# A layer with routed experts on one core: the first pair's first half ahead of its last rows, and the final sums tile by tile

## What is computed

```
h = x + concat(a, c) @ w_out                 # 1024 x 1024
xn = rms_norm(h, g_norm_ffn)
lg = xn @ w_router_group;  g = argmax(lg)    # 4 groups
le = xn @ w_router_expert                    # 8 experts in the group; the best two are taken
w_sel = softmax(top_v) * p_g
y = h + sum over the two experts of w_sel * (silu(xn @ w_gate[e]) * (xn @ w_up[e])) @ w_down[e]
```

## Time and profile before

| | us |
|---|---|
| median of 3 runs | 611.67 |
| lowest and highest | 610.62, 613.29 |
| the profiled execution's own time | 607.84 |
| its span, first to last instruction | 606.1 |
| TensorE busy in the span | 553.9 |
| VectorE, ScalarE, GpSimd busy | 278.1, 166.8, 119.2 |
| mean granted clock of TensorE | 0.965 |
| bytes moved by DMA | 163.48 MB |

### The profile page before, as it was taken

The page is one execution under the profiler, slowest core; times in us unless marked ns, Lnnn a source line. Parts: engine busy times, 40 slices in busy tenths (PEclk is TensorE's granted clock), DMA queues, the critical chain, the costliest instruction groups (busy, mean ns, idle before and its releaser), DMA issues.

```text
span 606.1 us, 8209 instructions
## 1 busy us (share of the span) xinstructions
PE 553.9 (91%) x2944; PEld 332.5 (55%) x2944; DVE 278.1 (46%) x681; ACT 166.8 (28%) x365; POOL 119.2 (20%) x124
## 2 busy tenths in 40 slices
PE   6999999998999999899999999999996869687992
PEld 4798899887675888744555853333332313232320
DVE  5887667968314787524358731111210111111256
ACT  7445344423312567610412210100100100000031
POOL 0488788310001000000000021111110111100013
PEclk9999999999999999899999999999997979898897
DMA  7990342599377900069600879999999999999874
GB/s 274 281 304 5 118 156 66 183 273 316 143 209 251 420 31 2 2 203 407 264 35 36 355 250 388 409 419 419 422 421 421 421 419 421 420 422 419 333 297 156
DMA packets 47159, 163.48 MB, mean 270 GB/s; under 512 B 8650, under 2 KB 22026, under 8 KB 35832
## 3 DMA queue, kind: packets, MB, share of 16 engines
q1 hardware_dynamic: 40448, 145.46, 63.2%
q0 software_dynamic: 6528, 17.01, 7.8%
q10 hardware_dynamic: 144, 0.52, 0.2%
HBM read 151.06 MB, written 19.76 MB: 282 GB/s over the span
## 4 chain that ended last, share of the span: by engine, by line
PE 47%; SPq 17%; DMA 11%; DVE 6%; POOL 3%; issue 3%; ACT 2%; POOLq 0%; DVEq 0%; ACTq 0%
SPq L512 11%; PE bank L1022 9%; PE bank L1085 9%; SPq L525 6%; DMA ring<-in_w_up_dram 5%; PE bank L1112 4%; PE bank L875 4%; DMA x<-q_rows 3%; PE bank L786 3%; PE bank L860 2%; DVE x L1445 2%; PE bank L808 2%; POOL ring L2139 2%; DMA hn_rows<-work 2%; PE bank L809 2%
## 5 line engine op out<-in xcount | busy, mean ns | idle before, releaser
L1085 PE MATMUL bank<-ring,work 128*64 128x512 f32 x512 | 122.8, 636 | 19.8 <-DMA ring<-in_w_up_dram 19.5
L1085 PEld LDWEIGHTS bank<-ring,work 128*64 128x64 f32 x512 | 39.6, 146 | 100.9 <-issue 87.1
L1445 DVE TENSOR_TENSOR work<-work,bank 128x256 f32<-128x256 f32 x16 | 6.7, 422 | 134.0 <-ACT work L1383 134.0
L1112 PE MATMUL bank<-ring,work 128*64 128x512 f32 x256 | 60.1, 612 | 7.6 <-ACT work L1387 7.6
L729 PE MATMUL bank<-split 128*128 128x384 f32 x192 | 66.1, 344 | 0.1
L730 PE MATMUL bank<-split 128*128 128x384 f32 x192 | 64.3, 335 | 0.0
L1022 PE MATMUL bank<-ring 128*128 128x512 f32 x96 | 42.6, 595 | 0.0
L1383 ACT ACTIVATE work<-bank 128x256 f32<-128x256 f32 x16 | 6.2, 385 | 128.2 <-PE bank L1085 128.2
L2139 POOL TENSOR_TENSOR ring<-ring 128x192 f32<-128x192 f32 (+1 forms) x40 | 38.8, 988 | 8.0 <-DVEq L1540 6.9
L1445 DVE TENSOR_TENSOR split<-ring,split 128x768 fp32r<-128x768 f32 (+1 forms) x35 | 37.3, 1099 | 6.4 <-PE bank L716 6.1
L1112 PEld LDWEIGHTS bank<-ring,work 128*64 128x64 f32 x256 | 17.3, 140 | 40.1 <-issue 28.7
(11 more groups left out here) (266 smaller groups left out, 832.9 us busy)
## 6 DMA issues: line engine op xcount, KB each, us to landing
ring<-in_w_down_dram SPq DMA_DIRECT2D x32, 1024.0 KB, 24.5
ring<-in_w_gate_dram SPq DMA_DIRECT2D x28, 1024.0 KB, 23.1
ring<-in_w_up_dram SPq DMA_DIRECT2D x28, 1024.0 KB, 25.2
ring<-in_w_in_dram SPq DMA_DIRECT2D x7, 1536.0 KB, 11.4
results<-work POOLq DMA_DIRECT2D x1, 4160.0 KB, 26.1
x<-in_x_prompt_dram SPq DMA_DIRECT2D x8, 512.0 KB, 13.1
ring<-in_w_out_dram SPq DMA_DIRECT2D x1, 4096.0 KB, 17.9
ring<-in_w_gate_dram SPq DMA_DIRECT2D x8, 512.0 KB, 13.2
```

Source lines behind the costliest of these rows:

```text
L1085: last = pe.matmul(bank[2][64 * h:64 * h + 64, :], xgT[:, k, 64 * h:64 * h + 64], gate_up[s][h][:, :, k, :], start=(k == 0), stop=(k == KD ...
L1112: last = pe.matmul(bank[4 + j][64 * h:64 * h + 64, :], hT[:, c, 64 * h:64 * h + 64], down[s][h][:, c, j * 512:(j + 1) * 512], start=(c == ...
L1445: return dve.tensor_tensor(out, a, b, op)
```

## The change

Six things, which belong together in two places.

1. `wout` is two tensors of 512 columns, loaded by two DMAs. The even groups g use only the first, so SP issues the first gate and up loads of pair 2 at `op_done` 18 and no longer at 19.
2. `hn[4]` lies at float 4096, not 3072. `tokens(0)` no longer waits for its store; the wait goes to those who first write `yo[0]`, which lies there (`result` on VectorE and ScalarE's copy, for pair 0).
3. The chunks 0 to 3 of all tiles go ahead. Then VectorE evacuates bank 0 and TensorE runs the first four chunks of pair 0; the chunks 4 to 7 and `tabulate` follow within `pair(0)`, ahead of its second half. `pick(2)` stands ahead of `choose(3)`.
4. x of tiles 1 and 2 is multiplied by the identity into PSUM (`own_row`): two products after pair 13, with four small ones (`keep_warm`) behind them, one ahead of pair 15's `pair_down`, one in the final sums. The holder's product is added in PSUM, and `add_sum` goes.
5. The final sums go tile by tile in the order 0, NT, 1, 2, 3, both halves of a tile together. ScalarE and GpSimd scale and add tiles 1 and 2 by halves.
6. The last tile's store is issued by ScalarE.

```diff
-        wout = cut(ring, 2 * SLOT, KD, D)
+        wout = [cut(ring, 2 * SLOT + j * 4096, KD, 512) for j in range(2)]
-        hn = [cut(work, at, D) for at in (0, D, 0, D, 3 * D)]
+        hn = [cut(work, at, D) for at in (0, D, 0, D, 4 * D)]
+        FINAL = [0, NT, 1, 2, 3]
+        SUM_BANKS = {0: (2, 3), NT: (4, 5), 1: (6, 7), 2: (0, 1), 3: (2, 3)}
...
+            sp.wait_ge(S["op_done"], 4 * NT + 2)
+            gates((4, 5), 2, (0,))
             sp.wait_ge(S["op_done"], 4 * NT + 3)
-            gates((4, 5), 2, (0,))
             downs((4, 5), 2)
...
                 for k in range(KD):
+                    if first and k == KD // 2:
+                        for m in range(1, T5):
+                            pick_rows(m, high_half)
+                        for b in range(len(GROUPS)):
+                            tabulate(b)
...
+            def own_row(t, half):
+                pe.matmul(sum_bank(t, half)[:, :], ident[:, :], x[:, t, half * 512:(half + 1) * 512], start=True, stop=False)
             for i in range(13, 16):
...
+                else:
+                    own_row(SUMMED[1], 0)
                 pair_down(i, s, i // 3 + 1, False, i == PAIRS - 1)
+                if i == 13:
+                    own_row(SUMMED[0], 0)
+                    own_row(SUMMED[0], 1)
+                    keep_warm(4, bank[3])
...
-            for half in range(2):
-                pe.wait_ge(S["dn_evac_v" if half else "dn_evac_a"], PAIRS)
-                for m, t in enumerate(LAST):
...
+            for m, t in enumerate(FINAL):
+                if t == SUMMED[1]:
+                    own_row(t, 1)
+                for half in range(2):
+                    if m == 0:
+                        pe.wait_ge(S["dn_evac_v" if half else "dn_evac_a"], PAIRS)
+                    if t == FINAL[-1]:
+                        pe.wait_ge(*((S["h_done"], T5 + 1) if half else (S["add_read"], 1)))
+                    pe.matmul(sum_bank(t, half)[0:TILES[t], :], holder[:, t, 0:TILES[t]], yo[0][:, half * 512:(half + 1) * 512],
+                              start=(t not in SUMMED), stop=True).then_inc(S["added"], 1)
...
-                if isinstance(i, int) and i == 0:
-                    dve.wait_ge(rows_moved[ORDER[NT]], 16)
...
             read_ranks(2)
+            pick(2)
             r_copy(4)
             choose(3)
-            pick(2)
             read_ranks(3)
             pick(3)
             place(2)
+            tokens(0, gains[:, 22:30], (0,))
             place(3)
...
-            tokens(0, gains[:, 22:30])
+            tokens(0, gains[:, 22:30], (1,))
...
+                if t in SUMMED:
+                    dve.wait_ge(S["back_summed"], 2 * SUMMED.index(t) + half + 1)
+                    rows = back[t][:, 0, cols]
+                else:
+                    rows = x[0:n, t, cols]
+                tt(x[0:n, t, cols], rows, sum_bank(t, half)[0:n, :], ALU.add).then_inc(S["h_done" if half else "add_read"], 1)
...
+            act.wait_ge(S["h_done"], 2 * T5)
+            act.dma_start(y_rows[FINAL[-1]], x[:, FINAL[-1], :]).then_inc(S["y_out"], 16)
```

More of the change, by code:

```diff
@@ L387, in placed, with sum_bank @@
             return first[m] + n
-        def add_bank(k):
-            return bank[(0, 1, 6, 7, 2, 3, 4, 5, 0, 1)[k]]
+        def sum_bank(t, half):
+            return bank[SUM_BANKS[t][half]]
         T5 = NT + 1
@@ L498, in _ @@
             sp.wait_ge(S["blk_done"], 6)
-            sp.dma_start(wout, w_out_v).then_inc(S["wout_in"], 16)
+            for j in range(2):
+                sp.dma_start(wout[j], w_out_v[:, :, j * 512:(j + 1) * 512]).then_inc(S["wout_in"], 16)
             sp.wait_ge(S["v_used"], 2)
@@ L909, in _ @@
                 last.then_inc(S["a_turned"], 1)
[L910 removed]
+            pe.wait_ge(S["wout_in"], 32)
             pe.wait_ge(S["a_evac"], 2 * NT + 1)
@@ L1003, in _ @@
                     q = k // 2
-                    last = pe.matmul(bank[6 + j][32 * q:32 * q + 32, :], mixsT[:, k, :], wout[:, k, j * 512:(j + 1) * 512],
+                    last = pe.matmul(bank[6 + j][32 * q:32 * q + 32, :], mixsT[:, k, :], wout[j][:, k, :],
                                      start=(k % 2 == 0), stop=(k % 2 == 1))
@@ L1021, in out_group @@
                         src = attnT[:, k, t * P:(t + 1) * P] if k < NP else yT[:, k - NP, t * P:(t + 1) * P]
-                        last = pe.matmul(bank[g][:, :], src, wout[:, k, cols], start=(k == rng[0]), stop=(k == rng[-1]))
+                        last = pe.matmul(bank[g][:, :], src, wout[g % 2][:, k, :], start=(k == rng[0]), stop=(k == rng[-1]))
                 last.then_inc(S["op_done"], 1)
@@ L1052, in _ @@
             route(4, (0,))
+            low_half, high_half = range(4), range(4, 8)
             pick_rows(0, range(0, 3))
@@ L1427, in _ @@
             for t in SUMMED:
-                for i in range(2):
-                    scaled_rows(t, i)
+                for half in range(2):
+                    for i in range(2):
+                        scaled_rows(t, i, slice(half * 512, (half + 1) * 512))
+            act.wait_ge(S["h_done"], 2 * T5)
+            act.dma_start(y_rows[FINAL[-1]], x[:, FINAL[-1], :]).then_inc(S["y_out"], 16)
             act.wait_ge(S["flag_ready"], 1)
@@ L1870, in h_root, with tokens @@
                 dve.wait_ge(S["h_root"], m + 1)
-            def tokens(i, gain=gain_f):
-                if isinstance(i, int) and i == 0:
-                    dve.wait_ge(rows_moved[ORDER[NT]], 16)
-                else:
+            def tokens(i, gain=gain_f, halves=(0, 1)):
+                if not isinstance(i, int) or i > 0:
                     dve.wait_ge(S["gu_done"], i)
-                for g in range(2):
+                for g in halves:
                     dve.wait_ge(S["xg_turned"], 2 * i + g + 1)
@@ L2012, in add_rows @@
                 return add_row(t, 1)
[L2014 to L2018 removed]
             def add_last(m, half):
[L2022 removed]
+                t = FINAL[m]
                 n, cols = TILES[t], slice(half * 512, (half + 1) * 512)
[L2024 to L2026 removed]
+                dve.wait_ge(S["added"], 2 * m + half + 1)
+                if t in SUMMED:
[4 more added lines that the diff above has]
+                tt(x[0:n, t, cols], rows, sum_bank(t, half)[0:n, :], ALU.add).then_inc(S["h_done" if half else "add_read"], 1)
             put, need = chain.put, chain.need
             rows = {NT: add_rows(NT), 0: add_rows(0)}
[L2030 removed]
+            for m, t in enumerate(FINAL):
+                if t == SUMMED[1]:
+                    rows[3] = add_rows(3)
                 if t in rows:
@@ L2213, in _ @@
             for n, t in enumerate(SUMMED):
-                pool.wait_ge(S["back_scaled"], 2 * n + 2)
-                pool.tensor_tensor(back[t][:, 0, :], back[t][:, 0, :], back[t][:, 1, :], ALU.add).then_inc(S["back_summed"], 1)
+                for half in range(2):
+                    pool.wait_ge(S["back_scaled"], 4 * n + 2 * half + 2)
+                    cols = slice(half * 512, (half + 1) * 512)
+                    pool.tensor_tensor(back[t][:, 0, cols], back[t][:, 0, cols], back[t][:, 1, cols], ALU.add)\
+                        .then_inc(S["back_summed"], 1)
             pool.wait_ge(S["flag_ready"], 1)
```

56 lines of the change are left out of this document (16 added, 40 removed).

## The result

| | before | after |
|---|---|---|
| median, same chip, 22 runs each (us) | 610.55 | 613.17 |
| lowest and highest | 607.01, 613.29 | 611.21, 615.61 |
| the profiled execution, its span | 607.84, 606.1 | 614.15, 612.4 |
| mean granted clock | 0.965 | 0.960 |

The ratio is 1.0044, interval 1.0029 to 1.0059: +2.7 us (+1.8 to +3.6). The forecast was 608.7 us and a range up to 612.8.

What follows compares the result with a forecast made beforehand. The weight stream sets the pace from pair 4 on, so earlier changes count by when it becomes continuous. Terms +2.9 - 2.7 - 3.2 = -3.0 us took 611.67 to 608.7 us; range 605.0 to 612.8.

Steps and rivals of the forecast that it cites:

- The first term: First pair: the weight stream becomes continuous later, at `gu_done` 2, costing +2.9 us; bounds +1.2 and +7.5.
- The second half: Pair 0 on TensorE: its second half ends at 360.6 us instead of 359.0, +1.6 us.
- The gather: Ahead of `turn_tokens(1)`: issued at 358.4, takes 3.7 us, lands at 362.1, and TensorE waits 1.5 us.
- The late gather: At `turn_tokens(1)`: a gather of 8.3 us makes the sum +1.6, 613.3 us; with 9.9, 614.9 us; chance 10%.
- the same work: From `turn_tokens(1)` to `gu_done` 2: the same work stands there, so the 3.1 us delay carries on to 378.2 us.
- My bounds for that step: At `pair_down(0)`: if the clock stays up, 1.7 us come back and the front costs +1.2.
- The second term: Pair 14: products filling TensorE's wait keep the clock up, 10.08 to 7.09 us, giving -2.7 us; bounds 0 and -3.0.
- The rival of a clock that falls all the same: Before pair 14: the clock falls despite the filled wait, sum -0.3, 611.4 us; chance 15%.
- The third term: Final sums: tile by tile, VectorE's adds end 2.9 us earlier and the last store gains 0.3, together -3.2 us.
- the near bound: Final sums: the smallest gain, -2.3 us, with adds of 3.50 us and one more GpSimd half block of 0.9.

Runs made afterwards that it cites:

- the front alone: Parts 1 to 3 of the change with the end as before, against the kernel before: +6.7 us, and +5.3 us when measured a second time.
- The old order: Kernels whose front is ordered as before: all eight chunks and the table ahead of pair 0. With the rest of the change: -2.1 us against before.
- 1 MiB less: Parts 4 to 6 on the old front, with the very last load of weights cut from 1 MiB to 8 KB: -4.4 us against before.
- the stores held: Parts 4 to 6 on the old front, SyncE's first result store held until the last of five result loads has landed: -1.6 us against before.
- the end alone: Parts 4 to 6 of the change with the old front, against the kernel before: -2.0 us.
- the new end with the front as it was: Parts 4 to 6 on the old front, without or with parts 1 and 2 of the change: -2.0 and -2.1 us against before.
- moving `weigh`: `weigh` put behind `pair_down(0)`: in the changed kernel +0.9 us against before; with new end, early loads and old front order -1.4 us.
- the table moved: Changed kernel with `tabulate` ahead of the 16 high chunks: +4.0 us against before; with VectorE's three table operations also ahead of `tokens(0)`: +2.2 us.
- the short tail: Parts 4 to 6 on the old front, expert 31's down matrix load cut to 8 KB: -4.4 us against before.

## Why the prediction was wrong

**The first term, +2.9, should have been +4.7 to +6** by the runs (the whole less its end, and the front alone). The mechanism was right: pair 0's first half came early, and it didn't matter; `gu_done` 2 set the start of the stream; lateness in front of it costs most of its length. The lateness was mis-sized, 3.1 us for 5.4 between the two profiled executions. By the steps of the forecast:

- The second half was to end at 360.6 and ended at 361.8 (364.96 less the 3.16 by which the store of `hn` was late): 1.2 us. 0.85 of them were lost before pair 0 began, where the chunks took 3.36 us for 2.03 with PEclk 0.50 at 345 to 348. The old order has this in five of its eight executions too, so it isn't the change's. In the second execution of the front alone the chunks are as quick as before (2.05), and there the second half ends 1.7 us later than before, where 1.6 was forecast.
- The gather was priced well: 3.55 us to landing and a wait of 1.17, where 3.7 and 1.5 stood. The late gather, which was my case on the slower side, didn't happen.
- Behind it I wrote "the same work", and this is the step that failed. The work was the same and its time wasn't: `weigh` +0.3, the two transposes +0.25, `pair_down(0)` +0.8, together 1.4 us, mostly at the lower clock (PEclk 0.52 at 370 to 376). In the second execution of the front alone they are again 1.4 us more. `pair_down(0)` took 5.14 to 5.35 us in the seven executions of the old order with `weigh` in its place, and 6.15, 5.45 and 6.41 in the three of the changed one. My bounds for that step had only a gain.

**The second term, -2.7, was 0.** Its first half held to the hundredth (7.09 us, 0.67 idle ahead), its second failed: "its scatter releases the loads of the results". I had seen that 8 MiB of weights would end at 578.2 and took 0.3 us off for it. But the scatter's rows landed with the end of these weights, whether it was issued 4 or 7 us ahead of that: 21.2 to 21.4 us from pair 14's start to the loads with all the weights, 18.8 with 1 MiB less. The weights end the stretch, as everywhere from pair 4 on. The 3.0 us were besides the price of one execution: pair 14 took 10.08 us there and 10.04 in one other, but 8.5 to 8.8 in the remaining four without the filler. The rival of a clock that falls all the same had the right sum for this term by a wrong mechanism.

The Trainium skill, DMA: Bandwidth & Descriptors, section "Queues, rings and completion order", says that a DMA engine takes its queues in turn, packet by packet. The trace agrees in kind: between 440 and 570 us of the kernel before, the scatters land in 7.8 to 8.4 us beside gate and up loads that take 22.6 to 31.8. The rule gives no price, but these scatters do, and I missed it: one issued 3 us earlier, some 7 us ahead of the end of the weights, could not be taken to land in the 3.8 us of the last one. The scatters of before between 440 and 570 us:

```profile
DMA to landing us min/median/max: 7.8/8.0/8.4
```

**The third term, -3.2, was -2.0.** Tile by tile did shorten the tail, from 22.0 us to 20.2 (20.6 in the changed kernel). From the first load to the end of the span it is 26.2 to 27.2 us in the seven executions with the old sums and 23.9 to 24.8 in the eight with the new, 2.2 less on average. What I left out: stores that begin earlier take bandwidth from the loads still under way, so the last load took 13.3 us to land, and 11.8 with the stores held. And the 3.0 us for tile 3's adds stand only while GpSimd is through; where the load came earlier, they met. Two slips stand in the recorded working: tile 1's second product is the sixth and not the eleventh behind 586.18 (six give its 591.8), and 3.50 for 3.0 with one more block of 0.9 makes the near bound -1.8, not -2.3. The -2.0 lies beyond the recorded bound and within the corrected one. The interval of the end alone, -3.4 to -0.6, doesn't exclude the -3.2.

**The sum.** -3.0 forecast, +2.7 measured: 1.8 or more from the first term, 2.7 from the second, 1.2 from the third. All three errors pointed the same way, since each term took what the change saves at its own place and left out who else uses the clock, the queues or the port there. By traces alone the three are about 4, 0 and -2.2. The range ended at 612.8 because no case of mine let the clock's gain and a part of the sums fail together with a dearer front.

The best version is the new end with the front as it was (608.11 and 608.24 in two forms), 2.0 us or 0.3% below before. What remains open: whether the front's slower clock at `weigh` and `pair_down(0)` comes from the wait ahead of it or from the changed mix of products; moving `weigh` moved the slow stretch in one kernel and not in the other, and with the table moved the slow stretch lay in the 16 chunks, while `weigh` and `pair_down(0)` took what they take in the old order (2.29 and 5.35 us in both kernels). And part of why the front alone measured 0.6 to 2 us more than the whole less its end.

## What to carry to other kernels

Where one stream of transfers bounds a kernel, count the bytes that it has moved at the point from which it is continuous; splitting the first consumer frees one buffer earlier, but if it makes the following releases later the queue runs dry between them. A faster engine at the end of the stream is worth nothing while its result lands only with the end of the stream: look up how long such a transfer takes beside the stream before counting a clock gain. And a term that is "the same work, later" should be given a bound on the side of loss, from the same instructions at the lower clock.

## What the runs showed of the hardware

- TensorE's clock fell to its lower level while it issued without a gap. With `tabulate` (20 instructions of 32 columns, 2.3 us) a little ahead, 16 chunk instructions took 3.78 and 3.63 us, and 2.05 where pair 0's first half stood there; PEclk was 0.54 at 356 to 363 us in the first of these. What makes it fall isn't shown: in the old order pair 0 follows `tabulate` at full clock (7.09 us). `pair_down(0)` took 1.5 to 2.8 us more than its 3.65 in all executions but one.
- An indirect scatter of 128 rows took 7.8 to 8.4 us to land beside the full stream, 6.9 us when it was issued 7 us ahead of the stream's end, and 3.8 us when issued 4 us ahead of it.
- VectorE's two adds with two inputs in SBUF took 2.60 us alone. Where they met GpSimd's (stores held), one instruction of each grew: GpSimd's second from 1.26 to 2.25 us, VectorE's second from 1.28 to about 2.2. With the short tail only VectorE's first grew, to 2.38, and GpSimd's two stayed at 2.49. The Trainium skill, SBUF — State Buffer, section "SBUF: two separate sides", has one of them hold a shared port pair for its whole instruction while the other waits. The trace agrees: each grew by 0.9 to 1.1 us, about what was left of the other's instruction (1.1 to 1.3).
- Unchanged code reached the same store up to 3.7 us apart between executions (327.42 to 331.16). The stretch from 140 to 160 us had the same busy time, 18.16 us, at a granted clock of 1.00 and of 0.91.
